# Down weights of two experts in one 4 MiB transfer: one wait for both buffers, in a mixture-of-experts loop on Trainium2

## What is computed

```python
def hier_moe(xn, w_gr, b_gr, w_er, b_er, w_gate, w_up, w_down):
    ...                      # top-1 group, top-2 experts in it, tokens sorted by expert
    def expert_block(args):
        tok_b, e = args
        xb = xpad[tok_b]
        h = jax.nn.silu(xb @ w_gate[e]) * (xb @ w_up[e])      # 1024 x 512 each
        return h @ w_down[e]                                  # 512 x 1024
    ...
    return y.reshape(bn, s, d).astype(xn.dtype)
```

## Time and profile before

| | |
|---|---|
| median of 3 runs | 1479.89 us (1479.34 to 1480.69) |
| the profiled execution | 1480.28 us |
| its span | 1478.5 us |
| PE busy | 1284.7 us, 87% |
| DMA moved | 531.32 MB, mean 359 GB/s |
| loads of gate/up | 32 of 4096 KB, median 20.1 us from issue to landing |
| loads of down | 32 of 2048 KB, median 21.7 us |
| chain that ended last | PE 52%, DMA 31%, DVE 11%, ACT 3% |

### The profile page before, as it was taken

One profiled execution on the slowest core, in us unless ns is written; L12 is line 12 of the kernel. 1 busy time (PEld: TensorE's weight loads), 2 busy tenths in 40 slices (PEclk: granted clock), 3 DMA queues, 4 the chain that ended last, 5 costly groups with the idle time before them and its releaser, 6 DMA issues.

```text
span 1478.5 us, 15345 instructions
## 1 busy us (share of the span) xinstructions
PE 1284.7 (87%) x5264; PEld 675.3 (46%) x5264; DVE 722.1 (49%) x1548; ACT 529.3 (36%) x1271; POOL 322.0 (22%) x310
## 2 busy tenths in 40 slices
PE   6987999899898989899999799999977767887776
PEld 6874433333333323488898444455423323333322
DVE  4174210010001001387877766667677766666744
ACT  4442211111111111455663344434543444444433
POOL 6810000000000000000000433344433434433330
PEclk9998999999999999999999999999988989989999
DMA  9563599999999999974334999999999999999995
GB/s 351 187 243 128 242 417 429 430 428 434 426 435 426 431 429 435 344 288 171 114 113 159 385 416 418 418 406 419 419 420 420 420 420 420 419 421 418 421 420 235
DMA packets 59575, 531.32 MB, mean 359 GB/s; under 512 B 11640, under 2 KB 13944, under 8 KB 15224
## 3 DMA queue, kind: packets, MB, share of 16 engines
q0 software_dynamic: 36864, 268.45, 43.9%
q1 hardware_dynamic: 22648, 262.09, 43.4%
HBM read 529.47 MB, written 1.97 MB: 359 GB/s over the span
## 4 chain that ended last, share of the span: by engine, by line
PE 52%; DMA 31%; DVE 11%; ACT 3%; issue 2%; POOL 1%; SPq 0%; POOLq 0%; ACTq 0%; DVEq 0%
PE bank L1837 17%; DMA ring_pair<-in_w_gate_up 16%; DMA held<-in_uv,row_of 15%; PE bank L1579 11%; PE bank L754 7%; PE bank L1798 2%; PE bank L1515 2%; PE bank L755 2%; PE bank L1420 2%; DVE held L2405 2%; PE bank L1782 1%; PE bank L1603 1%; PE bank L1713 1%; DVE ti L2362 1%; PE bank L1694 1%
## 5 line engine op out<-in xcount | busy, mean ns | idle before, releaser
L1837 PE MATMUL bank<-held,diags 128*128 128x512 f32 x1024 | 489.4, 633 | 116.9 <-ACT diags L1300 116.9
L2405 DVE SCALAR_TENSOR_TENSOR held<-held,bank 128x1024 f32<-128x1024 f32 x256 | 306.6, 1219 | 198.7 <-DMA held<-in_uv,row_of 198.5
L1837 PEld LDWEIGHTS bank<-held,diags 128*128 128x128 f32 x1024 | 200.6, 202 | 401.9 <-issue 217.0
L980 POOL DMA_INDIRECT held<-in_uv,row_of x256 | 241.7, 944 | 624.5 <-PE bank L1837 381.9
L1579 PE MATMUL bank<-ring_pair,x_blk 128*64 128x512 f32 x1024 | 236.1, 615 | 22.5 <-DMA ring_pair<-in_w_gate_up 20.9
L2113 DVE TENSOR_TENSOR hid<-bank,hid 64x512 f32<-64x512 f32 x32 | 22.2, 695 | 406.5 <-ACT hid L1119 406.5
L1579 PEld LDWEIGHTS bank<-ring_pair,x_blk 128*64 128x64 f32 x1024 | 73.1, 141 | 170.8 <-issue 146.3
L1295 ACT ACTIVATE gelus<-dots 128x1 f32<-128x1 f32 x256 | 51.2, 200 | 244.1 <-DVE held L2405 243.4
L1119 ACT ACTIVATE hid<-bank 64x512 f32<-64x512 f32 x32 | 18.8, 588 | 290.4 <-PE bank L1579 290.4
L1300 ACT ACTIVATE diags<-const,hidden 128x128 f32<-128x128 f32 x256 | 102.7, 401 | 47.3 <-PE bank L1837 40.2
L1515 PE MATMUL bank<-ring,hT 128*64 128x512 f32 x512 | 115.4, 593 | 1.2 <-ACT hT L1123 1.2
(11 more groups left out here) (359 smaller groups left out, 1281.8 us busy)
## 6 DMA issues: line engine op xcount, KB each, us to landing
ring_pair<-in_w_gate_up SPq DMA_DIRECT2D x32, 4096.0 KB, 20.1
ring<-in_w_down SPq DMA_DIRECT2D x32, 2048.0 KB, 21.7
ring<-in_w_in SPq DMA_DIRECT2D x14, 2048.0 KB, 11.5
ring<-in_w_out SPq DMA_DIRECT2D x4, 2048.0 KB, 8.2
ring<-in_w_q SPq DMA_DIRECT2D x4, 2048.0 KB, 7.9
held<-in_uv,row_of POOLq DMA_INDIRECT x256, 17.1
rel_bias<-rpb_wide SPq DMA_DIRECT2D x4, 512.0 KB, 15.1
ring<-in_w_proj_a SPq DMA_DIRECT2D x1, 2048.0 KB, 7.9
```

The lines of the kernel that those rows point to most:

```text
L980: pool.indirect_dma_start(held[b][:, :], None, dram["uv"], bass.IndirectOffsetOnAxis(ap=row_of[:, i:i + 1], axis=0)).then_inc(row_full[b], 16)
L1837: last = pe.matmul(bank[SUM_BANK[t] + half][:, :], diags[i % DIAGS][:, :], held[i % ROWS_HELD][:, D + half * 512:D + (half + 1) * 512], st ...
L2405: dve.scalar_tensor_tensor(held[b][:, 0:D], held[b][:, 0:D], 1.0, two_banks[X_BANKS[t]][:, :], ALU.mult, ALU.mult, accum_out=dots[:, i:i + ...
```

## The change

The down weights of a pair's two experts lie side by side in DRAM (a row of a partition holds both, 32 KB) and are loaded as one transfer of 4 MiB into slots 4 and 5. SP waits for `down_done >= 4 * pair`: the down products of both experts of the pair before. The order in SP's loop is then gate/up of the first expert, gate/up of the second, down of the pair. TensorE's down products of either expert wait for this one load. The function `with_gate` becomes `in_company`, which leaves out of the count of `ring_full` the entries that come with another. The twin branch is changed in the same way.

```diff
-        ring_pair = {s: at(...) for s in (MOE_SLOTS[0], MOE_SLOTS[3])}
+        ring_pair = {s: at(...) for s in (MOE_SLOTS[0], MOE_SLOTS[3], MOE_SLOTS[2])}
...
-        def with_gate(n):
-            return CH_MOE <= n < CH_IN2 and PAIR[(n - CH_MOE) % RING][1] == 1
+        def in_company(n):
+            return CH_MOE <= n < CH_IN2 and PAIR[(n - CH_MOE) % RING] in ((0, 1), (1, 1), (1, 2))
...
             def down(i, pair):
-                src = dram["w_down"][bass.ds(2 * pair + PAIR[i][0], 1)].rearrange("e p f -> p (e f)")
-                sp.dma_start(ring[W_SLOT[i]][:, :], src).then_inc(ring_full[W_SLOT[i]], 16)
-
-            for i in (0, 2, 5, 3):
+                src = dram["w_down"][bass.ds(pair, 1)].rearrange("e p f -> p (e f)")
+                sp.dma_start(ring_pair[W_SLOT[i]][:, :], src).then_inc(ring_full[W_SLOT[i]], 16)
+
+            for i in (0, 2, 3):
...
                 if kind == 2:
-                    sp.wait_ge(down_done, 4 * pair + 2 * j - 2)
+                    sp.wait_ge(down_done, 4 * pair)
                     down(i, pair)
...
             with sp.Fori(2, PAIRS) as pair:
                 reload(0, pair)
-                reload(5, pair - 1)
                 reload(3, pair)
                 reload(2, pair)
-            reload(5, PAIRS - 1)
...
+            def down_part(w, f, half):
+                first = CHUNK_COLS * (w - W_SLOT[2]) + f * D + half * 512
+                return ring_pair[W_SLOT[2]][:, first:first + 512]
...
                         last = pe.matmul(dst[half * BLOCK:(half + 1) * BLOCK, :], hidden_t[:, f, :],
-                                         ring4(w)[:, f, half * 512:(half + 1) * 512], start=(f == 0), stop=(f == 3))
+                                         down_part(w, f, half), start=(f == 0), stop=(f == 3))
...
                 def down(e, pair, j, first):
-                    pe.wait_ge(ring_full[W_SLOT[3 * j + 2]], pair_fill(pair, 3 * j + 2))
+                    pe.wait_ge(ring_full[W_SLOT[2]], pair_fill(pair, 2))
...
-        "w_down": by_partition(g["w_down"][0]),
+        "w_down": by_partition(g["w_down"][0]).reshape(PAIRS, 2, P, -1).transpose(0, 2, 1, 3).reshape(PAIRS, P, -1),
```

More of the change, by code:

```diff
@@ L233, in build @@
         ring = [at(f"ring{s}", [P, CHUNK_COLS], ARENA + 16384 * s) for s in range(RING)]
-        ring_pair = {s: at(f"ring_pair{s}", [P, 2 * CHUNK_COLS], ARENA + 16384 * s) for s in (MOE_SLOTS[0], MOE_SLOTS[3])}
+        ring_pair = {s: at(f"ring_pair{s}", [P, 2 * CHUNK_COLS], ARENA + 16384 * s) for s in (MOE_SLOTS[0], MOE_SLOTS[3], MOE_SLOTS[2])}
         def gate_up8(s):
@@ L588, in former @@
             return max([i for i in range(n) if slot_of(i) == slot_of(n)], default=CH_OUT1 - 1)
-        def with_gate(n):
-            return CH_MOE <= n < CH_IN2 and PAIR[(n - CH_MOE) % RING][1] == 1
+        def in_company(n):
+            return CH_MOE <= n < CH_IN2 and PAIR[(n - CH_MOE) % RING] in ((0, 1), (1, 1), (1, 2))
         def landed(n):
-            return 16 * sum(slot_of(i) == slot_of(n) and not with_gate(i) for i in range(n + 1))
+            return 16 * sum(slot_of(i) == slot_of(n) and not in_company(i) for i in range(n + 1))
         def ring_wait(eng, n):
@@ L1523, in many_products @@
                         w_g, w_u, w_d = W_SLOT[3 * j:3 * j + 3]
-                        for kind in (0, 2):
-                            pe.wait_ge(ring_full[W_SLOT[3 * j + kind]], pair_fill(pair, 3 * j + kind))
+                        pe.wait_ge(ring_full[W_SLOT[3 * j]], pair_fill(pair, 3 * j))
+                        pe.wait_ge(ring_full[W_SLOT[2]], pair_fill(pair, 2))
                         for b in range(BLOCKS_MAX):
```

## The result

The changed kernel takes 1558.25 us (median, 1555.31 to 1560.96), the kernel before 1480.29 beside it: a ratio of 1.0506, with a 95% interval of 1.0481 to 1.0531 (the quotient of the two medians, 1.0527, lies in it). It is 78 us slower. The forecast was 1574.5 with a range of 1546 to 1595, slower with a chance of 0.94.

A forecast was written before the change was run, and what follows sets the result against it. DMA was taken as the bound (share 1.00, 430 GB/s). Pair 2 at 213.5 plus 13 periods of 35.4 gives 673.7 against 582.02, + 91.7; ends + 2.9; 1480.3 + 94.6 - 0.4 = 1574.5 us, range 1546 to 1595.

The forecast's parts named there:

- the DMA is dry until then: In each pair, the DMA engines would be empty from 8.5 to nearly 12 us after its start, counted as 3.3 us.
- Both loads from an empty queue: Down load plus next gate/up load, 8.39 MB issued 10.7 us into each pair: 22.8 us, bounds 21.9 and 23.2.
- just this case: Two down loads queued behind a gate/up load at the stage's start, issue 86.7 to landing 109.5: 22.8 us.
- the sum of 12.1 and 9.75: Low bound for the two loads: one load's landing time on an empty queue plus the second's bytes, 21.9 us.
- an upper bound of 0.45 us for a boundary between transfers: Possible cost between two transfers, at most 0.45 us each, 7 us for sixteen; the forecast took 0.
- The 2.0 us on each DMA: Skill's fixed cost per DMA; paid in series, sixteen fewer would save an estimated 32 us; the prediction said the trace disagrees.
- The slow start: First gate/up products of each pair at half clock after TensorE's gap: 1.9 us per pair, bounds 1.4 and 2.9.
- Pair 2 starts: Pair 2 would start 33.5 us after pair 1's 179.96, at 213.5, with no slow start before it.
- The end, from pair 15 on: The last pair's own slow start (1.9) and small wait (about 1): + 2.9 us.
- The small wait for down weights: In a pair's second expert, down products wait 0.3 to 1.6 us for their load, within time TensorE would idle anyway.
- half of 2.35: Landing comes about 1.3 us behind a load's last byte, half of the 2.35 us a single load has beside its bytes.
- That the clock holds (1548): Rival for the loop: same cycle, no slow start, period 33.5, 1548 us, or 1535 with low bound 32.6; chance 0.18.

The follow-up runs named there:

- experiment 1: Kernel before, two 2 MiB down transfers in the old layout, both issued only after both down products of the pair before: 1582.58 us, ratio 1.0679.
- experiment 2: Changed kernel with both down products of a pair done at its end, ahead of the next gate/up products, load still joined: 1485.11 us; again 1483.21.
- experiment 3: Changed kernel with SP issuing the next pair's first gate/up load ahead of the down load: 1574.20 us, ratio 1.0633.
- experiment 4: Changed kernel with five extra 128x512 products ahead of each pair's first gate/up products from pair 2 on: 1535.96 us, ratio 1.0362.
- its repeated run: The changed kernel unaltered, run once more: 1557.68 us, ratio 1.0509.
- experiment 5: Changed kernel with one 4 MiB down transfer but the old weight layout, two 16 KB rows for each partition: 1585.12 us, ratio 1.0687.
- experiment 9: As experiment 2, but down weights as two 2 MiB transfers with 16 KB rows, issued together behind the pair's down products: 1483.85 us, ratio 1.0008.

## Why the prediction was right

Its mechanism held step by step. The down load is released 10.7 us into the pair plus the slow start (12.5 at 225.84), the gate/up load stands behind it, the DMA is dry until then, both loads take a fixed time from an empty queue, TensorE idles and restarts at 1.2 GHz. Experiments 1 to 4 each take hold of one link. The wait alone gives the whole loss and more. An earlier release takes 73 us of it away. SP's order only moves the wait. The clock is 22 us of it, by the run that keeps it up; the other 56 are put down to the dry DMA by difference: with the clock kept up a pair is 32.58 us, before the change it was 28.72, 14 x (32.58 - 28.72) = 54, and 2 elsewhere.

*The terms.* By the two profiled spans the change cost 1559.5 - 1478.5 = 81.0 us, against 94.6 in the sum.
- Both loads from an empty queue: 22.8 us in the sum, 22.0 measured on average (21.8 to 22.2), next to the low bound of 21.9, 14 times. That is the mis-sized term: 12 us. I preferred a row of "just this case", taken where the stage begins, over the sum of 12.1 and 9.75. But that place is slow whatever is loaded there: in the changed kernel, with 4 MiB of long rows, the same two loads took 23.3 (issue at 85.46, landing at 108.7), and 22.7 in its repeated run. It was a row of another place. Nothing else was being loaded there: from 86.6 to 109.5 the kernel before moved 367 GB/s, 8.40 MB, which are the two loads' own bytes. Why this place is slower than the loop is open.
- From this the prediction also took an upper bound of 0.45 us for a boundary between transfers. Experiments 5 and 9 show none.
- The 2.0 us on each DMA of the Trainium skill, "DMA: Bandwidth & Descriptors", Anatomy of one DMA, an estimated 32 us in all, don't appear as a sum over transfers: with joined loads and a full queue (experiment 2) the pair is 0.08 us shorter than with two (experiment 9).
- The slow start: 1.9 us in the sum, 1.7 measured (8.78 on average of 14 pairs, from 8.52 to 10.10), 13 times: 3 us. All 14 gaps of 5.5 us led to one. In the repeated run of the same kernel the average was 8.55, 3 us less in all, so this term varies from run to run, as the kernel's times do (1555 to 1561).
- Pair 2 starts 32.4 us after pair 1, in the sum 33.5; the later start of pair 1 (180.90, against 179.96) was not in the sum, 0.9 us. The end, from pair 15 on: 1.9 us more than before, in the sum 2.9.
- The small wait for down weights: at most 0.7 us, in the sum 0.3 to 1.6, off the path as said.
- A slip: half of 2.35 is 1.2 us, not 1.3, for the landing behind the last byte. The bytes ended 8.8 us into the pair (8.5 in the prediction), the first new ones moved 1.0 us behind the issue, and the dry time is 4.7 us in place of 3.3, since the slow start puts the issue off by 1.8 us.

*What it had said to look for.* Landing of the down loads 12.3 us (12 to 13), of the gate/up loads 21 and 19.5 (22.5 and 20.5, the load term again), DMA share 0.86 and 366 GB/s (0.83, 355), wait of L1581 77.2 us (85). Loads 0.35 us apart were 0.9: between them SP turns its loop, which does no harm, as the load ahead takes 10 us.

*The rivals.* That the clock holds (1548) lies 10 us from the result, nearer than the forecast (16). The time alone would have chosen wrongly; the granted clock, the 8.8 us products and experiment 4 decide. Where the clock does hold, it measured 1536, which is this rival with the low bound for the loads (1535). The two errors, one in each term, went the same way, so neither hid the other.

## What to carry to other kernels

Two buffers that are freed one after the other are a queue of depth two; joined into one load, they are released at the time of the later one, and what counts is whether the transfers still queued at that moment last until the new one starts. Read the release from the issuing queue's timeline, the end of the queued bytes from the DMA share by the microsecond, and charge the dry time once per turn, plus the slow restart of TensorE if its gap grows. If a joined load is wanted, first move the last reader ahead. And a term that is taken 14 times should be taken from inside the loop, or summed from parts, not from one row of another place in the kernel, however alike the two look.

## What the runs showed of the hardware

- Five useless products in an idle gap made the kernel 22 us faster: with the gap at 1.0 us the granted clock stayed at 1.00 (2.4 GHz), with 5.5 us it was 0.50 (1.2 GHz) at every restart, and the following 7.1 us of products took 8.5 to 10.1. Gaps between these went either way: 2.1 us in experiment 9, 2.54 to 2.67 in the kernel before.
- A slow start costs time only where something waits behind it. With the DMA at a share of 1.00 the pairs of experiment 9 were 29.2 to 29.3 us long with and without one; where the next load is issued behind it, keeping the clock up was worth 22 us.
- The same 4 MiB land 12.3 us behind the issue with rows of 32 KB, 13.4 with 16 KB and 12.5 with 8 KB, when the queue had run dry. With a full queue the 16 KB layout costs nothing (430 GB/s).
- A transfer to 64 of the 128 partitions keeps the DMA engines at a share of 1.01 and moves 210 GB/s. A busy share of 1.00 is no proof of full bandwidth.
